# Six weight places in tile 0's projection, and attention of tiles 1 to 3 by single heads

## The reference

```python
h = rms_norm(x, norm_mix); q, k, v, u, g = split(h @ w_in)          # 5 parts of 1024
q, k = rms_norm over each of 8 heads of 128
for each block i of 128 queries:                                   # strictly causal
    z = q[i] @ k[:end].T * 128**-0.5
    log_rem = where(s < t, log_sigmoid(-z), 0)
    tail = reversed cumsum(log_rem) - log_rem
    w = where(s < t, exp(log_sigmoid(z) + tail), 0);  y_a[i] = w @ v[:end]
u, g = gelu(u), gelu(g)
y_b = u * (masked sg_w @ rms_norm(g) + sg_b)                        # gMLP, 8 groups, blocks of 128
x = x + concat(rms_norm(y_a), rms_norm(y_b)) @ w_out
x = x + peer(rms_norm(x))   # 16384 one-neuron experts: 8 heads choose 16 each by product keys
```

## Time and profile before

| | |
|---|---|
| runs | 3139.42, 3149.39, 3155.55 us; median 3149.39 |
| the profiled execution | 3142.57 us, span 3140.8 us |
| busy in the span | PE 2915.1, DVE 2205.6, POOL 1536.9, ACT 1175.4 us |
| DMA | 291 GB/s of HBM traffic over the span |
| granted clock of PE | 0.965 of full speed |

### The profile page before, as it was taken

The page is one execution under the profiler, slowest core; times in us unless marked ns, Lnnn a source line. Parts: engine busy times, 40 slices in busy tenths (PEclk is TensorE's granted clock), DMA queues, the critical chain, the costliest instruction groups (busy, mean ns, idle before and its releaser), DMA issues.

```text
span 3140.8 us, 43159 instructions
## 1 busy us (share of the span) xinstructions
PE 2915.1 (93%) x17829; PEld 2748.0 (87%) x17829; DVE 2205.6 (70%) x3093; ACT 1175.4 (37%) x1387; POOL 1536.9 (49%) x630
## 2 busy tenths in 40 slices
PE   6899899966998999998899799999999999999998
PEld 5687788844887999998899799999999999999998
DVE  5656476755586679997777566667677677777876
ACT  6755532335323333333333333333333233333331
POOL 0000263311142358882223577777765776677662
PEclk9999999987998999999999899999999999999999
DMA  7746538943697866766778988888989999999996
GB/s 300 277 161 256 213 134 337 341 151 134 246 345 268 303 248 228 242 226 229 282 249 285 347 344 342 344 344 337 352 331 358 358 364 366 359 366 354 360 360 219
DMA packets 189564, 915.75 MB, mean 292 GB/s; under 512 B 16944, under 2 KB 76448, under 8 KB 86464
## 3 DMA queue, kind: packets, MB, share of 16 engines
q1 hardware_dynamic: 102320, 485.79, 42.0%
q0 software_dynamic: 56112, 406.05, 33.4%
q10 hardware_dynamic: 31008, 22.29, 2.2%
HBM read 872.31 MB, written 41.68 MB: 291 GB/s over the span
## 4 chain that ended last, share of the span: by engine, by line
PE 60%; DVE 16%; DMA 14%; ACT 4%; issue 2%; ACTq 1%; POOL 1%; SPq 1%; DVEq 0%; POOLq 0%
PE ps L1555 12%; PE ps L1864 7%; PE ps L1866 6%; PE ps L1865 6%; DMA g_in<-gelu_scratch 5%; PE ps L1795 5%; PE ps L1796 5%; PE ps L1797 5%; PE ps L1780 4%; PE ps L1542 3%; DVE ring_lo L1040 3%; DVE rows L1253 2%; DVE ps L1263 2%; PE ps L1838 2%; DMA rows<-peer_u_rows,idx_far 2%
## 5 line engine op out<-in xcount | busy, mean ns | idle before, releaser
L558 POOL TENSOR_TENSOR ring_lo<-ring_raw,ring_hi 128x2048 fp32r<-128x2048 f32 x217 | 1040.9, 4798 | 774.7 <-ACT ring_hi L633 773.2
L633 ACT ACTIVATE ring_hi<-ring_raw 128x2048 fp32r<-128x2048 f32 x400 | 763.1, 1915 | 731.3 <-DMA ring_raw<-peer_u 213.1
L1864 PE MATMUL ps<-a_hi,ring_hi 128*128 128x320 f32 x2048 | 639.6, 312 | 32.9 <-DVE a_lo L1405 25.8
L1795 PE MATMUL ps<-bT_hi,ring_hi 128*128 128x320 f32 x2048 | 646.9, 316 | 21.0 <-DVE ring_lo L1040 9.3
L1796 PE MATMUL ps<-bT_lo,ring_hi 128*128 128x320 f32 x2048 | 639.3, 312 | 0.0
L1797 PE MATMUL ps<-bT_hi,ring_lo 128*128 128x320 f32 x2048 | 638.9, 312 | 0.0
L1865 PE MATMUL ps<-a_lo,ring_hi 128*128 128x320 f32 x2048 | 635.5, 310 | 0.0
L1866 PE MATMUL ps<-a_hi,ring_lo 128*128 128x320 f32 x2048 | 635.2, 310 | 0.0
L1040 DVE TENSOR_TENSOR ring_lo<-ring_raw,ring_hi 128x2048 fp32r<-128x2048 f32 x183 | 448.3, 2459 | 263.8 <-ACT ring_hi L633 263.8
L586 POOL DMA_INDIRECT rows<-peer_u_rows,idx_far x128 | 224.1, 1751 | 494.2 <-DVE z_far L1253 455.1
L1864 PEld LDWEIGHTS ps<-a_hi,ring_hi 128*128 128x128 f32 x2048 | 386.3, 189 | 42.7 <-DVE a_lo L1405 26.4
(11 more groups left out here) (288 smaller groups left out, 3823.5 us busy)
## 6 DMA issues: line engine op xcount, KB each, us to landing
ring_raw<-peer_u SPq DMA_DIRECT2D x128, 1024.0 KB, 5.8
ring_raw<-peer_v SPq DMA_DIRECT2D x128, 1024.0 KB, 6.9
ring_raw<-w_in SPq DMA_DIRECT2D x80, 1024.0 KB, 4.9
ring_raw<-w_out SPq DMA_DIRECT2D x32, 1024.0 KB, 4.9
ring_raw<-w_query SPq DMA_DIRECT2D x32, 1024.0 KB, 5.2
g_pair<-gates_scratch SPq DMA_DIRECT2D x64, 320.0 KB, 7.6
gelu_scratch<-ahead ACTq DMA_DIRECT2D x72, 160.0 KB, 5.3
g_in<-gelu_scratch SPq DMA_DIRECT2D x72, 160.0 KB, 7.3
```

The costliest lines, as they stand in the source:

```text
L558: pool.tensor_tensor(ring_lo[s][:], ring_raw[s][:], ring_hi[s][:].bitcast(F32), ALU.subtract)\
L633: act.activation(ring_hi[place(n)][:], ring_raw[place(n)][:], ACT.Copy).then_inc(hi_ok[SLOT[n]], 1)
L1795: pe.matmul(dst, hi[:, e], bT_hi[:, k, 0:NEAR], start=(k == 0), stop=False)
L1864: pe.matmul(dst, hi[:, col], a_hi[:, par, e, :], start=(e == 0), stop=False)
```

## The change

Two things are changed.

First, the ring. Two more places are laid out in memory which is still unused while tile 0 is projected (at 60 and 76 KB, under bT_hi and bT_lo). Pieces 0 to 35 go round six places; the semaphores stay by the old four slots. So a load waits for the piece that last lay in its place to be freed (PREV_AT: n-6 here), and, in tile 0's projection, for the high part of the piece with the same semaphores (n-4).

Second, attention of tiles 1 to 3. The pairs are dissolved: PE runs `values_of(n-2)`, the two transposes of head n+2, `scores_of(n+1)` and `tails_of(n)` in one step n; ACT `weights(n-1)`, `copy_y(n-2)`, the copies of head n+2, and abs, exp, ln of head n+1; DVE `block_z(n-1)`, `norm_qk(n+3)`, two rows (none in the last step), and `keep_sp(n+1)`. The gMLP goes into steps 0 to 3, two groups each (`norm_v`, `mix`, `gate_u`), in banks 0 and 7. The statistics are inverted at piece 108 instead of behind piece 111. The low parts of pieces 112 and 113 are no longer made inside the loop; they are made where the loop over pieces 112 on asks for them, behind `turn_lo_b` on DVE. The six squares of the last pair's step are spread over the last steps and behind them.

```diff
+WIDE_END = 36
+PLACE = [5 + n % 6 - 4 if n < WIDE_END and n % 6 >= 4 else n % 6 if n < WIDE_END else 4 if SLOT[n] == 3 and n >= AHEAD
+         else SLOT[n] for n in range(N_PIECES)]
+PREV_AT = [max([m for m in range(max(0, n - 200), n) if PLACE[m] == PLACE[n]], default=-1) for n in range(N_PIECES)]
...
@@ -89,7 +94,8 @@
        [("u2", s) for s in range(G2)] + [("v2", s) for s in range(G2)]
 N_ROWS = len(ROWS)
 ROWS_AT = [0] * N_PIECES
-ATTEND_ROWS = (4, 4, 4, 2)
+
+ATTEND_ROWS = (2, 2, 2, 2, 2, 2, 2, 0)
...
-    places = (0, 16, 32, 164, 96)
+    places = (0, 16, 32, 164, 96, 60, 76)
...
     def place(n):
-        return 4 if SLOT[n] == 3 and n >= AHEAD else SLOT[n]
+        return PLACE[n]
...
+        def z_of(n):
+
+            first = 1 + 3 * (n % 2)
+            return ps[:, first:first + 3, :].rearrange("p b n -> p (b n)")
+
+        def y_bank(n):
+            return 7 * (n % 2)
+
+        def turn_bank(n, j):
+            return 7 * ((n + 1 + j) % 2)
+
+        def mix_bank(h):
+
+            return 7 * ((h // 2 + 1 + h) % 2)
...
-                    if USE[n] > 1:
-                        sp_eng.wait_ge(freed[SLOT[n]], USE[n] - 1)
+                    before = PREV_AT[n]
+                    if before >= 0:
+                        sp_eng.wait_ge(freed[SLOT[before]], USE[before])
+                    if n < IN_B0 and USE[n] > 1:
+
+                        sp_eng.wait_ge(hi_ok[SLOT[n]], USE[n] - 1)
...
-            act.wait_ge(st_var, 3)
-            st = statB.rearrange("p s t h -> p (s t h)")
-            act.activation(st, st, ACT.Sqrt).then_inc(st_root, 1)
...
+                elif c == 8:
+                    act.wait_ge(st_var, 3)
+                    st = statB.rearrange("p s t h -> p (s t h)")
+                    act.activation(st, st, ACT.Sqrt).then_inc(st_root, 1)
+
+
+            def copy_qk(n, j):
+                act.wait_ge(qk_turned, 2 * n + j + 1)
+                act.activation(qkT[:, n % 2, j, :], ps[:, turn_bank(n, j), 0:NB], ACT.Copy, scale=(qgain, kgain)[j])\
+                   .then_inc(qkT_out, 1)
...
+            def softplus_parts(n):
+                z = z_of(n)[:, 0:1152]
+                act.wait_ge(z_done, n + 1)
+                act.activation(sp_t[:, n % 2, :], z, ACT.Abs).then_inc(z_step, 1)
+                act.wait_ge(z_step, 2 * n + 1)
+                act.activation(sp_t[:, n % 2, :], sp_t[:, n % 2, :], ACT.Exp, scale=-1.0).then_inc(z_step, 1)
+                act.wait_ge(z_step, 2 * n + 2)
+                act.activation(sp_t[:, n % 2, :], sp_t[:, n % 2, :], ACT.Ln, bias=1.0).then_inc(z_ln, 1)
+
+            def weights(n):
+                act.wait_ge(z_blocked, 2 * n + 2)
+                act.activation(w_att[:, n % 2, :], z_of(n)[:, 0:1152], ACT.Exp).then_inc(w_made, 1)
+
+            def copy_y(n):
+                act.wait_ge(pv_done, n + 1)
+                act.activation(projB[Q_PART][:, :, n * HD:(n + 1) * HD],
+                               ps[:, y_bank(n), 0:NB].rearrange("p (t c) -> p t c", t=TB), ACT.Copy).then_inc(y_out, 1)
...
+            for n in range(2):
+                copy_qk(n, 0)
+                copy_qk(n, 1)
+            softplus_parts(0)
+            for n in range(HEADS):
+                if n:
+                    weights(n - 1)
+                if n >= 2:
+                    copy_y(n - 2)
+                if n + 2 < HEADS:
+                    copy_qk(n + 2, 0)
+                    copy_qk(n + 2, 1)
+                if n + 1 < HEADS:
+                    softplus_parts(n + 1)
+                if n >= HEADS - TB:
                     act.wait_ge(gated, HEADS)
-                if i < TB:
-                    square_y(1, i, i + 1)
-                else:
-                    for t in range(TB):
-                        act.wait_ge(row_sq[MIX_NORM_B], TB + t + 1)
-                        act.activation(junkB[:, 0:768], projB[Q_PART][:, t, 0:768], ACT.Square,
-                                       accum_out=ss_part[:, t:t + 1]).then_inc(row_sq[MIX_NORM_B], 1)
-                for ab in range(2):
-                    n = 2 * i + ab
-                    act.wait_ge(pv_done, n + 1)
-                    act.activation(projB[Q_PART][:, :, n * HD:(n + 1) * HD],
-                                   ps[:, 7 * ab, 0:NB].rearrange("p (t c) -> p t c", t=TB), ACT.Copy).then_inc(y_out, 1)
+                    square_y(1, n - HEADS + TB, n - HEADS + TB + 1)
+            for t in range(TB):
+                act.wait_ge(y_out, HEADS - 2)
+                act.wait_ge(row_sq[MIX_NORM_B], TB + t + 1)
+                act.activation(junkB[:, 0:768], projB[Q_PART][:, t, 0:768], ACT.Square,
+                               accum_out=ss_part[:, t:t + 1]).then_inc(row_sq[MIX_NORM_B], 1)
+            weights(HEADS - 1)
+            copy_y(HEADS - 2)
+            copy_y(HEADS - 1)
...
+                if n == 108:
+                    invert_stats(statB.rearrange("p s t h -> p (s t h)"), SQ_B[7])
...
-            invert_stats(statB.rearrange("p s t h -> p (s t h)"), SQ_B[7])
-            dve.wait_ge(s_sgp, 64)
-            dve.memset(sgwB[64:128, :, 0:64], 0.0).then_inc(s_sgm, 1)
-            dve.wait_ge(in_out_b, 30)
-            for h in range(HEADS):
+            wait_piece(dve, OUT_B - 1)
+
...
-                if i == 0:
-                    lo_upto(OUT_B + 1)
-                rows_step(ATTEND_ROWS[i] - 2)
+
+            def keep_sp(n):
+                dve.wait_ge(z_ln, n + 1)
+                sp_n = sp[:, n % 2, :]
+                dve.scalar_tensor_tensor(out=sp_n, in0=z_of(n)[:, 0:1152], scalar=0.0, in1=sp_t[:, n % 2, :],
+                                         op0=ALU.max, op1=ALU.add).then_inc(sp_made, 1)
+                dve.wait_ge(sp_made, n + 1)
+                two = sp_n[:, 384:640].rearrange("p (b n) -> p b n", n=P)
+                dve.tensor_tensor(two, two, bcast(keep[:], [P, 2, P], 1), ALU.mult).then_inc(sp_kept, 1)
+                dve.tensor_tensor(sp_n[:, 896:1024], sp_n[:, 896:1024], keep[:], ALU.mult).then_inc(sp_kept, 1)
+
+            def block_z(n):
+                dve.wait_ge(tails, n + 1)
+                z = z_of(n)
+                two = z[:, 384:640].rearrange("p (b n) -> p b n", n=P)
+                dve.tensor_tensor(two, two, bcast(block_m[:], [P, 2, P], 1), ALU.add).then_inc(z_blocked, 1)
+                dve.tensor_tensor(z[:, 896:1024], z[:, 896:1024], block_m[:], ALU.add).then_inc(z_blocked, 1)
+
+            norm_qk(0)
+            norm_qk(1)
+            dve.wait_ge(in_out_b, 30)
+            dve.wait_ge(s_sgp, 64)
+            dve.memset(sgwB[64:128, :, 0:64], 0.0).then_inc(s_sgm, 1)
+            norm_v(0)
+            norm_v(1)
+            norm_qk(2)
+            keep_sp(0)
+            for n in range(HEADS):
+                if n:
+                    block_z(n - 1)
+                if n + 3 < HEADS:
+                    norm_qk(n + 3)
+                rows_step(ATTEND_ROWS[n])
+                if n < HEADS // 2:
+                    gate_u(2 * n)
+                    gate_u(2 * n + 1)
+                    if n < HEADS // 2 - 1:
+                        norm_v(2 * n + 2)
+                        norm_v(2 * n + 3)
+                if n + 1 < HEADS:
+                    keep_sp(n + 1)
+            block_z(HEADS - 1)
...
-            pe.wait_ge(s_sgm, 3)
+
             pe.wait_ge(in_out_b, 30)
             pe.wait_ge(rq_inv, 1)
...
+            def turn_qk(n, j):
+                pe.wait_ge(qk_normed, 2 * n + j + 1)
+                for t in range(TB):
+                    last = pe.transpose(ps[:, turn_bank(n, j), t * P:(t + 1) * P], qk_n[:, n % 2, j, t, :], ident[:])
+                last.then_inc(qk_turned, 1)
+
+            def mix(h):
                 pe.wait_ge(vb_made, TB * (h + 1))
-                pe.matmul(ps[:, h, 0:NB].rearrange("p (t c) -> p t c", t=TB), sgwB[:, h, :],
+                pe.matmul(ps[:, mix_bank(h), 0:NB].rearrange("p (t c) -> p t c", t=TB), sgwB[:, h, :],
                           projB[G_PART][:, :, h * HD:(h + 1) * HD], start=True, stop=True).then_inc(mixed, 1)
-
...
+            def scores_of(n):
+                z = z_of(n)
+                pe.wait_ge(qkT_out, 2 * n + 2)
+                if n >= 2:
+                    pe.wait_ge(w_made, n - 1)
+                fresh = {0, 512, 1024}
...
+                last.then_inc(z_done, 1)
+
+            def tails_of(n):
+                z = z_of(n)
+                pe.wait_ge(sp_kept, 2 * n + 2)
...
+                last.then_inc(tails, 1)
+
+            def values_of(n):
+                pe.wait_ge(w_made, n + 1)
+                for t in range(1, 4):
...
+            turn_qk(0, 0)
+            turn_qk(0, 1)
+            for j in range(2):
+                pe.wait_ge(qkT_out, 2 - j)
+                turn_qk(1, j)
+            scores_of(0)
+            for n in range(HEADS):
+                if n >= 2:
+                    pe.wait_ge(gated, min(2 * n, HEADS))
+                    if n > HEADS // 2:
```

(21 more changed lines are left out.)

139 lines of the change are left out of this document (26 added, 113 removed).

## The result

The changed kernel takes 3114.07 us (median of 4 runs, 3103.42 to 3124.82), the kernel before 3150.47 beside it: ratio 0.9886, 95% interval 0.9860 to 0.9913. I had stated 3108 us, and 3092 to 3132 as range. The profiled execution took 3112.47 us, its span is 3110.0.

What follows compares the result with a forecast made beforehand. Tile 0's projection was held by the ring of four and ACT's order, with neither PE nor DMA full; attention by latency. Gains 10.9 + 34.4 - 5.5 = 39.8 us took 3149.4 to 3109.6; stated 3108, range 3092 to 3132.

Steps and rivals of the forecast that it cites:

- Stage 1: Tile 0's input projection: with six ring places the stage ends 10.9 us earlier, bounds 0 and 16.
- The second term: Tile 0's projection, pieces 10 to 27: PE's work counts, 49.1 us, plus 4.1 for two clock falls; done at 114.3.
- Statistics at piece 108: Inverting the statistics at piece 108 instead of behind 111: DVE waits about 3 us, cost 0, bounds 0 and 3.
- Prologue: Start of attention, from piece 111's end near 651 to the first block_z at 678.8: 20 us gained, bounds 16 and 23.
- The term from there on: Before the first block_z: DVE's norm 1.0, two rows 4.4, gates and norm_v 2.7, keep_sp 2.0, block_z 0.7 us.
- Head cycle: Attention of tiles 1 to 3: 12.1 us per steady head, 13.8 for heads 4 to 6 with clock falls; 77.0 altogether.
- The rival with a fall in every head: Attention: the clock falls in heads 1 to 6, 15.6 us each; gain only 23 us, 3126; chance 0.10.
- Table loads: ACT in attention: two per head, 1.28 us each without a drain; only ln's is on the chain, inside the 12.1.
- End of attention: Behind block_z(6): weights, values and copy of head 7 end 9.5 us later, at 765.3; 34.4 us gained.
- The lost cover of lo(112): Start of the output projection: PE waits 3.8 us for lo(112), plus 1.7 for the clock: -5.5, bounds -2 and -6.
- The slow rival: Attention: two row gathers in series ahead of keep_sp make a head 24 us, total 3176, slower than before; chance 0.03.
- outside them I expect the program to run as before, only earlier: Everything but tile 0's projection and attention of tiles 1 to 3: unchanged, since waits are on events; size 0.

Runs made afterwards that it cites:

- e3_lo_back: The changed kernel with the low parts of pieces 112 and 113 made behind the last block_z, ahead of the norm: 3112.47 us, ratio 0.9890.
- e7_prologue: e3_lo_back with head 0's two row gathers moved to head 7 and head 2's q,k norm ahead of the mixing-weights wait: 3095.26 us, one run.
- e5_filled_idle: e3_lo_back with 8 dummy matmuls in PE's idle time ahead of head 7's second turn and ahead of its scores: 3091.81 us, one run.
- e9_order: e5_filled_idle with ACT's weights of head 7 and copy of head 6 ahead of three squares: weights 6 to first turn of y 14.14 us, before 14.01.
- e10_x0b_spread: e5_filled_idle with the edits of e7_prologue and e9_order, and x0B loaded in three 1 MiB parts behind pieces 13, 17, 21: 3083.76 us, ratio 0.9806.
- e2_attention_only: The changed kernel with pieces 0 to 35 in the old four places, so only attention is new: 3127.89 us, ratio 0.9941.
- e6_x0b_late: e3_lo_back with x0B (3 MiB) loaded after piece 11, not 7, and its squares moved to evacuation 2: tile 0's projection ends at 177.9 us.

## Why the prediction was right

The range held the time, and the stated 3108 is 6 us low. Both changed stages gain by the mechanisms forecast. That the number came so close is in part luck: the stages gave 6.6 us more than forecast, and the rest of the program, put at no change, took about 10 back (46.4 at 900 us, 36.4 in the medians).

- **Stage 1, 10.9 us forecast, 11.4 measured.** The right sum from partly wrong terms. Piece 9 landed at 45.04, not 42.3: DMA had moved 17.0 MB by then (378 GB/s over 45.04 us) and not the 15.7 of the sum, since pieces 10 and 11, in flight sooner, share it. From that landing to piece 10 it took 14.1 us, through ACT's high part, evacuation and squares, as forecast; so piece 10 started at 59.13 (56.4), 2.7 late. The idle time ahead of it was 4.09, not 7: I had PE done with pieces 8 and 9 at 49.4, but 8 itself waited until 46.97. The second term was off the other way: before piece 18 PE idled 1.63 us and not 2.06, the clock stayed up, and piece 30 started at 126.94 (126.6). That ACT's order would be the bound that is left holds before 10, behind a late landing, and before 30.
- **Statistics at piece 108, cost 0.** DVE waits 0.33 us for ACT's root there and not about 3. The lead went from 12.2 us at 600 to 10.3 at the end of piece 111 in this trace, by waits for gathered rows; in others it rose.
- **Prologue, first `block_z` 27.8 us behind piece 111.** 24.8 measured. Scores of head 0 started 4.2 us behind the piece, not 5.9, and took 1.97 us at the full clock, not 2.9 at 1.2 GHz. That is this execution's good luck: in e3_lo_back, with those scores at 3.07 us, it is 26.5, and in the kernel's own second trace 26.8, where the chain went through the landing of sgnB and head 1's scores took 3.85. The term from there on, DVE's order with two rows in it, was right, as e7_prologue shows by taking them away.
- **Head cycle.** 11.53 us where the sum gave 12.1 (the second turn 0.55 for 0.8, most other terms a little less). The clock fell in three heads as forecast, but in 1, 5 and 6 and not in 4 to 6. Head 1 took 12.35 us for 11.4: its scores, behind 3.97 us of idle time, took 3.62. Heads 5 and 6 took 13.2 and 12.2 us for the 13.8 charged, the fall 1.7 and 1.2 of it. From the first to the seventh `block_z` 72.3 us, forecast 77.0. e5_filled_idle shows that the idle time makes the fall, and its price: 2.9 us over three heads. The rival with a fall in every head, at 15.6 us each, is out: three heads, the longest 13.2.
- **Table loads.** 1.28 us each, the next activation 0.01 us behind (684.50 and 685.80 above). The Trainium skill ("ScalarE: Activation LUTs", What ACT_TABLE_LOAD costs) has 1.38 us of drain on top; by that page the head would be 12.9 us, an estimate, and 11.53 was measured. No run here shows the drain.
- **End of attention, 9.5 us behind `block_z(6)`.** Measured 9.6. From the end of piece 111 to this point 41.9 us are gained, forecast 34.4.
- **The lost cover of lo(112).** Wait 3.61 (3.8), in all 6.2 (5.5); e3_lo_back takes it all away.
- **The slow rival**, row gathers in series, needed a head of 19.5 us: DVE waited for a row twice in the heads, 0.92 us at 669.73 and 0.32 at 715.14.

So at 900 us the lead was 46.4 and the forecast 39.8. The step that failed is the first one, "outside them I expect the program to run as before, only earlier". The new attention's program has stalls of PE in the last stage that the kernel before shows in neither of its traces, 4.0 us in this one. And the same program's lead varies by more than the forecast's error: between 1050 and 1134 us and behind 1640 it went from 46.5 to 30.8 in one execution and from 41.0 to 18.4 in another. A rule that an earlier start is given back doesn't stand: e5_filled_idle, e9_order and e10_x0b_spread, which have no such stall, keep 50.8, 50.6 and 60.1 us to the end. How much a mean over many executions would lose there, and to what beside the stalls, stays open: the medians give 36 and 40 us for the changed kernel where its own stages show 44 to 49.

## What to carry to other kernels

When a load is brought forward, ask first whether DMA has room at that moment: 3 MiB moved within a saturated stretch moved the idle times, the same 3 MiB spread to where PE is the bound removed most of them. A stage limited by a chain through four engines is gained head by head from the rows of one cycle, and what the old loop hid under itself (here two low parts) has to be given a new place by name. Short idle times of PE on such a chain cost twice, and dummy matmuls that wait for an event just ahead of the idle time remove the second part. When a total moves and no stage that was touched does, look for idle time without a wait and at the packets of the instruction queue. And before an effect of 3 us is explained, the same kernel's second trace should be read.

## What the runs showed of the hardware

- The granted clock stayed up behind idle times of 1.23 and 1.63 us and fell behind 2.52, 2.56 and about 5. The length of one idle time alone doesn't decide it: in e2_attention_only one of 2.52 us was followed by a turn of 0.55, at the full clock; 2.02 us at 103.77 in e10_x0b_spread did no harm, 2.06 before piece 18 in the kernel before did. How long it stays down varies: 12.5 to 13.9 us for the same 96 matmuls behind the same idle time.
- One core's DMA held 423 GB/s over 20 us with 1 MiB loads and one of 3 MiB; PE then idled 4.7 us for the next piece's landing (4.6 in e6_x0b_late).
- PE stood still for 3.9 to 4.8 us without waiting for any event, nine times in six traces, each with nine more packets in the instruction queue (83 for 74 in the changed kernel).
- Executions of one program differ by up to 9 us in one stretch of 84 us (1050 to 1134), with nothing changed.
